# Forming each eight-block product of the late program in two halves, placed separately between the pairs of rows

## The chip, the cores and the metric

One core of one Trainium2 chip. The metric is the device time of one execution in microseconds (us). The engines are TensorE (PE for its matmuls, PEld for its weight loads), VectorE (DVE), ScalarE (ACT), GpSimd (POOL) and SyncE (SP), which issues most of the direct transfers.

## What is computed

One layer of an encoder over 1024 tokens of width 1024, all in fp32. What matters here is its last part, the "late" stage:

```
merged = sigmoid(gate_r) * (y_r @ w_proj_ret) + sigmoid(gate_s) * (y_s @ w_proj_sgu) + sigmoid(gate_a) * (y_a @ w_proj_att)
h = h + merged @ w_out
# PEER: 8 heads, 16 experts of 16384 for each head and token
act = gelu(einsum('thkd,td->thk', u_tab[eid], xt)); w = gate * act
h = h + einsum('thk,thkd->td', w, v_tab[eid])
h = h + sigmoid(rms_norm(h) @ ple_gate) * (p @ ple_proj)
```

The gates, `w_out`, the queries of PEER and `ple_gate` are products over a depth of 1024, which is eight blocks of 128.

## The kernel before

The 1024 tokens are eight tiles of 128, in three groups: tiles 0 and 1, tiles 2 to 4, tiles 5 to 7. Two earlier stages prepare keys and branches; then `late_stage` runs to the end and takes most of the time.

**Rows.** For each tile there are 128 selected experts for every token (8 heads times 16). One *row* r is one of these 1024 selections: GpSimd gathers 8 KB for each of the 128 tokens (`u` and `v` of the expert, 1 MB in all) into one of SLOTS = 11 buffers (L1218). VectorE forms the dot product with `u` (L1669), ScalarE the weight from it (L1493, L1497), and the weighted `v` is added either by VectorE (L1679) or by TensorE (L1344, four matmul records for a row, with a diagonal matrix made by ScalarE at L1501). TENSOR_ROWS says which: on TensorE 4 of 8 rows for tiles 0 and 1, 5 of 8 for tiles 2 to 4, 6 of 8 for tiles 5 to 7. GpSimd may gather row r only when row r - 11 has been added (`acc_done` or `acc2_done`), in the order of the rows.

**Slots.** `Plan` writes the order of every engine by hand. The late program is a list of slots; two rows, a *pair*, belong to each slot from `plan.first` = 35 on, so pair g is slot 35 + g, and there are 512 pairs. The dense products are *jobs*, each placed in a slot. In slot s each engine does, in this order:

- TensorE: the weighing (L1344) of pair s - 1, then the jobs of slot s.
- ScalarE: its part of the jobs of slot s - 1 (it reads their PSUM banks), its part of the search, then the weights of pair s.
- VectorE: its part of the jobs of slot s - 1 (`merge` L1585 and others), the dots of pair s, its weighing of pair s - 1, `finish` and `output` of a tile, then a part of the search (`search_keys` twice, `search_pairs`, `choose`, once in each eight slots).
- SP: the loads and stores whose conditions fall in slot s, in one queue.

A job of kind vs, us, gate, out, query or pgate has two chunks of weights of 1 MB each (`n_chunks` = 2) and takes eight blocks, all formed at one place by `matmuls` (L117, sixteen matmul records). A proj has one chunk and four blocks. The chunks stand in a ring of RING = 4 buffers; chunk n is loaded when the last job that uses chunk n - 4 has ended.

**Placement.** Up to the first rows, jobs are packed by PROLOGUE_US = 6.5 for each slot. Behind that `place` advances a position `at` by `job.us / rate[job.g]`, with `job.us` = 6.9 for an eight-block product and 3.5 for a proj; worked out, the rates are 6.5 for what is left of the first group, 3.99 for each slot in the second group and 2.45 in the third. `earliest` holds some kinds back by the slot of another job. The last products of a tile (hturn, pproj, pgate: `place_ple`, "the closing jobs of a tile" below) come after its last row, six slots for each tile.

Of the kernel before, what the change touches and what calls it, by code (L numbers as in the profile page):

```python
# [23 lines left out]
P = 128  # L24
S, D = 1024, 1024
T = S // P
DC = D // P
# [736 lines left out]
ACCS = 3  # L764
# [9 lines left out]
class Job:  # L774

    def __init__(self, kind, us, at, n_pa, n_pb, chunk, n_chunks, g=None, i=None, n=None, half=None, j=None, y=None, t=None):
        self.kind, self.us, self.at, self.slot = kind, us, at, None
        self.n_pa, self.n_pb, self.chunk, self.n_chunks = n_pa, n_pb, chunk, n_chunks
        self.pa, self.pb = (), ()
        self.g, self.i, self.n, self.half, self.j, self.y, self.t = g, i, n, half, j, y, t  # L780


class Plan:
# [22 lines left out]
    def count(self):  # L806

        self.jobs.sort(key=lambda job: job.slot)
        self.at = [[] for _ in range(self.n_slots)]
        n_pa = n_pb = 0  # L810
        for job in self.jobs:
            job.pa, n_pa = tuple(range(n_pa, n_pa + job.n_pa)), n_pa + job.n_pa
            job.pb, n_pb = tuple(range(n_pb, n_pb + job.n_pb)), n_pb + job.n_pb
            for k in range(job.n_chunks):
                self.last_job[job.chunk + k] = job
            self.at[job.slot].append(job)

    def take(self, source, *indices):
# [60 lines left out]
    def place(self):  # L879

        slot, used = 0, 0.0
        jobs = iter([job for job in self.jobs if job.t is None])
        start = self.of["score", 0, 1]
        for job in jobs:
            if used >= PROLOGUE_US or job.kind == "xt":
                slot, used = slot + 1, 0.0
            if self.earliest(job) > slot:
                slot, used = self.earliest(job), 0.0
            job.slot = slot
            used += job.us  # L890
# [12 lines left out]
        for job in rest:  # L903
            if job.g == 2:
                at = max(at, float(begin))
            at = max(at, float(self.earliest(job)))
            job.slot = int(at)
            at += job.us / rate[job.g]
        self.end = self.first + PAIRS
        self.n_slots = self.end + 10  # L910
        self.place_ple()
# [11 lines left out]
    def place_ple(self):  # L923

        free = 0
        for t in range(T):
# [3 lines left out]
            for half in range(2):  # L930
                self.of["pproj", t, half].slot = slot + 2
                self.of["pgate", t, half].slot = slot + 3 + half
            free = slot + 6

# [19 lines left out]
def late_stage(nc, A, R, X):  # L954


    plan = Plan()
    with ExitStack() as ctx:
# [66 lines left out]
        row_in = [sem(f"row{n}_in") for n in range(SLOTS)]  # L1025
        wp_in, pt_in, out_done = sem("wp_in"), [sem(f"pt{n}_in") for n in range(2)], sem("out_done")
        pa_done, pb_done = sem("pa_done"), sem("pb_done")
# [29 lines left out]
        def _(sp):  # L1057
# [72 lines left out]
            def load_h(t):  # L1130

                g = [n for n, group in enumerate(GROUPS) if t in group][0]
                i = GROUPS[g].index(t)
                sp.wait_ge(h_out[i], (nth(g, i) - (i < K0)) * 16)
                wait(sp, out_done, (t - ACCS + 1) * 32)
                sp.dma_start(acc[:, t % ACCS, :], X["h"][t]).then_inc(acc_in[t % ACCS], 16)
# [12 lines left out]
            def store_half(t, half):  # L1149
                hs = slice(half * HB, (half + 1) * HB)  # L1150
                sp.wait_ge(out_ready, 2 * t + half + 1)
                sp.dma_start(A["out"][t][:, hs], sum_of(t)[:, hs]).then_inc(out_done, 16)

# [14 lines left out]
            for s in range(plan.n_slots):  # L1168
# [30 lines left out]
                for n in range(len(PLE_TILES)):  # L1199
                    if s == plan.of["score", n + 1, 4 * len(GROUPS[n + 1]) - 1].slot + 1:  # L1200
                        load_wp(n)
            sp.wait_ge(out_done, T * 32)

# [23 lines left out]
        def _(pe):  # L1227
# [15 lines left out]

            def gate(job):
                if job.i == 0:
                    loaded(pe, job.chunk)
                    loaded(pe, job.chunk + 1)
                if job.kind == "vs":
                    wait(pe, xg_in[job.i], (nth(job.g, job.i) - (job.i < len(GROUPS[0]))) * 16)
                matmuls(pe, into_pa(job.pa[0])[:], [(xt[:, job.i, c * P:(c + 1) * P], wide_chunk(job.chunk, c)) for c in range(DC)]).then_inc(pa_done, 1)  # L1250

# [29 lines left out]

            def out(job):
                if job.i == 0:
                    loaded(pe, job.chunk)
                    loaded(pe, job.chunk + 1)
                for n in plan.of["turn", job.g, job.i].pb:
                    freed_pb(pe, n)
                matmuls(pe, into_pb(job.pb[0])[:], [(mt(job.i)[:, c * P:(c + 1) * P], wide_chunk(job.chunk, c)) for c in range(DC)]).then_inc(pb_done, 1)

# [3 lines left out]

            def query(job):
                if job.i == 0:
                    loaded(pe, job.chunk)
                    loaded(pe, job.chunk + 1)
                for n in plan.of["xt", job.g, job.i].pb:
                    freed_pb(pe, n)
                x = turned(job.g, job.i)  # L1300
                matmuls(pe, into_pa(job.pa[0])[:], [(x[:, c * P:(c + 1) * P], wide_chunk(job.chunk, c)) for c in range(DC)]).then_inc(pa_done, 1)

# [25 lines left out]

            def gate_product(job):
                loaded(pe, job.chunk)  # L1330
                loaded(pe, job.chunk + 1)
                for n in plan.of["hturn", job.t].pb:
                    freed_pb(pe, n)
                matmuls(pe, into_pa(job.pa[0])[:], [(ht[:, c * P:(c + 1) * P], wide_chunk(job.chunk, c)) for c in range(DC)]).then_inc(pa_done, 1)

            def weigh(r):
# [5 lines left out]
                for half in range(2):  # L1342
# [4 lines left out]
            query_of = {job.y: job for job in plan.jobs if job.kind == "query"}  # L1347
            qturn_of = {job.y: job for job in plan.jobs if job.kind == "qturn"}
            programs = {"vs": gate, "us": gate, "mix": mix, "yst": turn_gated, "gate": gate, "proj": proj, "turn": turn, "out": out, "xt": turn_normed, "query": query, "qturn": turn_query, "score": score,
                        "hturn": turn_sum, "pproj": project, "pgate": gate_product}  # L1350
# [481 lines left out]
```

## Time and profile before

| | |
|---|---|
| median of 3 runs | 3784.19 us (3777.92 to 3784.67) |
| the profiled execution's own time | 3773.32 us |
| its span | 3771.5 us |
| TensorE busy, share of the span | 82% |
| VectorE busy | 71% |
| bytes moved by DMA | 1281.06 MB, mean 340 GB/s |
| mean granted TensorE clock | 0.918 |

The span is that of the profiled execution, from the first to the last instruction. The dots (L1669) tell where a pair stands in time. Counted by them, these pairs begin at these times of the span:

| pair | 0 | 16 | 32 | 64 | 72 | 80 | 120 | 144 | 240 | 256 | 304 | 328 | 448 | 456 | 504 |
|---|---|---|---|---|---|---|---|---|---|---|---|---|---|---|---|
| us | 838.7 | 956.7 | 1052.3 | 1272.5 | 1326.0 | 1387.1 | 1621.8 | 1781.6 | 2322.5 | 2414.8 | 2677.9 | 2826.1 | 3423.0 | 3471.7 | 3703.7 |

The second group's gates and projections lie in pairs 20 to 68, its out products in 70 to 79; the closing jobs of tiles 0 and 1 in 120 to 132; the third group in 136 to 297, its out products in 234 to 250; the closing jobs of tiles 2, 3 and 4 in 305 to 324, those of tiles 5, 6 and 7 in 385 to 388, 449 to 452 and behind the last pair.

### The profile page before, as it was taken

To read this page: it belongs to the slowest core of one execution; us is meant where nothing else is said; L and a number is where in the kernel's file an instruction comes from. 1 tells how busy PE (TensorE), PEld (TensorE's weight loads), DVE (VectorE), ACT (ScalarE), POOL (GpSimd) and SP (SyncE) were. 2 spreads that over 40 slices of the span, in tenths; PEclk is the share of its full clock that TensorE was granted. 3 is DMA by queue.
4 is the path that set the end of the run, shared out by engine and by line. 5 is a ranking of instruction groups with operands and counts; after the bars stand their busy time and mean duration, and the time that the engine had idled before them with its cause. 6 is when DMAs were issued, how large, how long until landed. Compare 5 with 4: busy or idle time off the path is not lost. (4 is left out here: it accounts for less than half of the span.)

```text
span 3771.5 us, 31162 instructions
## 1 busy us (share of the span) xinstructions
PE 3078.5 (82%) x7880; PEld 1410.6 (37%) x7880; DVE 2671.1 (71%) x5254; ACT 1365.1 (36%) x3576; POOL 1198.4 (32%) x1092
## 2 busy tenths in 40 slices
PE   7889998988988989768988888798787677677676
PEld 4545554433433334323433333343332223223222
DVE  4356663136868778777888887877778878878884
ACT  3223332023443333344434433433453334334332
POOL 0000000013433334333544433443335444444442
PEclk9989998998999999888999999999898889889888
DMA  3321113459999999999999999999999999999996
GB/s 138 103 97 41 48 34 131 154 202 421 404 394 361 390 396 425 423 399 398 425 426 427 426 426 419 395 425 424 420 350 423 426 427 419 426 427 400 425 427 266
DMA packets 207881, 1281.06 MB, mean 340 GB/s; under 512 B 24048, under 2 KB 37616, under 8 KB 61936
## 3 DMA queue, kind: packets, MB, share of 16 engines
q0 software_dynamic: 147456, 1073.81, 68.7%
q1 hardware_dynamic: 55232, 195.61, 13.6%
q10 hardware_dynamic: 5040, 9.96, 0.7%
q8 instruction: 51, 0.84, 0.1%
q14 instruction: 102, 0.84, 0.1%
HBM read 1250.98 MB, written 28.31 MB: 339 GB/s over the span
## 5 line engine op out<-in xcount | busy, mean ns | idle before, releaser
L1344 PE MATMUL l_acc<-l_rows,l_diag 128*128 128x512 f32 x2624 | 1415.9, 684 | 600.3 <-ACT l_diag L1501 587.2
L1218 POOL DMA_INDIRECT l_rows<-in_peer_uv,l_at x1024 | 1177.7, 1150 | 1696.5 <-DVE l_acc L1679 846.0
L1344 PEld LDWEIGHTS l_acc<-l_rows,l_diag 128*128 128x128 f32 x2624 | 535.6, 214 | 1415.9 <-ACT l_diag L1501 857.1
L1669 DVE SCALAR_TENSOR_TENSOR l_rows<-l_rows,l_xn 128x1024 f32<-128x1024 f32 x640 | 762.9, 1223 | 142.3 <-DMA l_rows<-in_peer_uv,l_at 109.9
L1669 DVE SCALAR_TENSOR_TENSOR l_rows<-l_rows,all_xt 128x1024 f32<-128x1024 f32 x384 | 460.3, 1224 | 148.4 <-DMA l_rows<-in_peer_uv,l_at 125.0
L1493 ACT ACTIVATE l_dots<-l_dots 128x2 f32<-128x2 f32 x512 | 103.7, 203 | 1036.4 <-DVE l_rows L1669 1034.5
L1679 DVE SCALAR_TENSOR_TENSOR l_acc<-l_rows,l_wts,l_acc 128x1024 f32<-128x1024 f32 x272 | 349.5, 1285 | 98.2 <-ACT l_wts L1497 98.0
L117 PE MATMUL l_pa<-all_ring,all_xt 128*128 128x512 f32 x688 | 310.6, 603 | 4.5 <-PEq L71 4.5
L1497 ACT ACTIVATE l_wts<-l_dots,l_gates 128x1 f32<-128x1 f32 x1024 | 293.5, 287 | 16.8
L117 PE MATMUL l_pa<-l_ring,all_xt 128*128 128x512 f32 x656 | 293.8, 599 | 0.0
L1211 POOL CAST l_at<-l_expert 128x16 uint32<-128x16 f32 x64 | 20.5, 320 | 831.0 <-DVE l_expert L1655 830.8
L1501 ACT ACTIVATE l_diag<-all_ident,l_wts 128x128 f32<-128x128 f32 x656 | 263.5, 402 | 21.5
L117 PEld LDWEIGHTS l_pa<-all_ring,all_xt 128*128 128x128 f32 x688 | 133.8, 195 | 172.4 <-issue 172.4
L495 PE MATMUL b_p<-mix_w_branches,b_xnt 128*128 128x512 f32 x384 | 185.1, 636 | 10.5 <-DMA b_xnt<-kept_xnt 10.5
L117 PEld LDWEIGHTS l_pa<-l_ring,all_xt 128*128 128x128 f32 x656 | 126.5, 194 | 157.6 <-issue 157.6
L1493 ACT ACT_TABLE_LOAD x125 | 160.4, 1283 | 42.5 <-DVE l_rows L1669 41.3
L117 PE MATMUL l_pb<-l_ring,l_yt 128*128 128x512 f32 x320 | 144.6, 601 | 0.0
L117 PE MATMUL l_pb<-all_ring,l_yt 128*128 128x512 f32 x320 | 143.1, 597 | 0.0
L1679 DVE SCALAR_TENSOR_TENSOR l_merged<-l_rows,l_wts,l_merged 128x1024 f32<-128x1024 f32 x96 | 123.1, 1282 | 15.8 <-ACT l_wts L1497 15.8
L1390 ACT ACTIVATE l_sgk<-l_pa 128x512 f32<-128x512 f32 x48 | 28.7, 597 | 244.0 <-PE l_pa L117 243.9
L495 PEld LDWEIGHTS b_p<-mix_w_branches,b_xnt 128*128 128x128 f32 x384 | 76.5, 206 | 105.1 <-issue 86.8
L1629 DVE MAX8 l_top<-l_s_in 128x8 f32<-128x128 f32 x256 | 74.7, 292 | 41.0 <-DMA l_s_in<-kept_s 36.4
(262 smaller groups left out, 2893.1 us busy)
## 6 DMA issues: line engine op xcount, KB each, us to landing
l_ring<-in_w_late SPq DMA_DIRECT2D x54, 1024.0 KB, 9.0
all_ring<-in_w_late SPq DMA_DIRECT2D x54, 1024.0 KB, 8.8
l_rows<-in_peer_uv,l_at POOLq DMA_INDIRECT x1024, 17.3
kept_s<-l_yt ACTq DMA_DIRECT2D x32, 256.0 KB, 7.7
l_s_in<-kept_s SPq DMA_DIRECT2D x64, 128.0 KB, 7.0
mix_w_branches<-in_w_branches_kept SPq DMA_DIRECT2D x8, 768.0 KB, 4.8
k_x<-in_x SPq DMA_DIRECT2D x8, 512.0 KB, 6.0
k_w<-in_w_keys SPq DMA_DIRECT2D x2, 2048.0 KB, 10.7
```

Of the source, the lines that this page charges most:

```text
L117: last = pe.matmul(out, lhsT, rhs, start=(n == 0), stop=(n == len(pairs) - 1))
L495: last = pe.matmul(out[:], xnt[:, c, :], R["w_branches"][:, c, column:column + HB], start=(c == 0), stop=(c == DC - 1))
L1211: pool.tensor_copy(at[:, c % 2, :], expert[:, c % 3, :]).then_inc(at_ready, 1)
L1218: pool.indirect_dma_start(out=rows[:, r % SLOTS, :], out_offset=None, in_=A["peer_uv"], in_offset=bass.IndirectOffsetOnAxis(ap=at[:, c % 2 ...
L1344: ins = pe.matmul(acc2[:, hs], diag[n_pe(r) % DIAGS][:], rows[:, r % SLOTS, D + half * HB:D + (half + 1) * HB], start=first, stop=last)
L1390: act.activation(sg(job.i), pa[job.pa[0] % 2][:], ACT.Sigmoid).then_inc(pa_free[job.pa[0] % 2], 1)
L1493: act.activation(dots[:, n:n + 2], dots[:, n:n + 2], ACT.Gelu).then_inc(act_done, 1)
L1497: ins = act.mul(wts[:, m:m + 1], dots[:, m:m + 1], gates[:, c % 3, m:m + 1])
L1501: act.mul(diag[n_pe(r) % DIAGS][:], R["ident"][:], wts[:, m:m + 1]).then_inc(diag_ready, 1)
L1629: order(dve.max(values[:, eight], scores))
L1669: dve.scalar_tensor_tensor(out=u, in0=u, scalar=1.0, in1=xn_of(t), op0=ALU.mult, op1=ALU.mult, accum_out=dots[:, n:n + 1]).then_inc(dot_do ...
L1679: dve.scalar_tensor_tensor(out=sum_of(t), in0=rows[:, r % SLOTS, D:2 * D], scalar=wts[:, n:n + 1], in1=sum_of(t), op0=ALU.mult, op1=ALU.ad ...
```

## The change

Each eight-block job behind the first rows has a second place, `head`: its first four blocks, with the first chunk, are issued in slot `head`, its last four, with the second chunk, in `slot`. Where both fall in one slot the job is formed whole. `at` advances by half of the job's `us` for each half. In a slot the second halves are issued before the first ones. Whatever reads the product, releases its chunks or counts from its slot goes by `slot`, that of the second half. The closing jobs of a tile take eight slots in place of six. The count of finished output stores becomes one semaphore for each of the three `acc` buffers.

```diff
@@ Plan.count
+        for job in self.jobs:
+            if job.head is not None and job.head < job.slot:
+                self.tails[job.slot].append(job)
+                self.heads[job.head].append((job, True))
+            else:
+                self.heads[job.slot].append((job, False))
@@ Plan.place
-            job.slot = int(at)
-            at += job.us / rate[job.g]
+            if job.n_chunks == 2:
+                job.head = int(at)
+                at += job.us / 2 / rate[job.g]
+                job.slot = int(at)
+                at += job.us / 2 / rate[job.g]
+            else:
+                job.slot = int(at)
+                at += job.us / rate[job.g]
         self.end = self.first + PAIRS
-        self.n_slots = self.end + 10
+        self.n_slots = self.end + 12
@@ Plan.place_ple
-                self.of["pgate", t, half].slot = slot + 3 + half
-            free = slot + 6
+                self.of["pgate", t, half].head = slot + 3 + 2 * half
+                self.of["pgate", t, half].slot = slot + 4 + 2 * half
+            free = slot + 8
@@ SP
-                wait(sp, out_done, (t - ACCS + 1) * 32)
+                wait(sp, out_done[t % ACCS], t // ACCS * 32)
-                sp.dma_start(A["out"][t][:, hs], sum_of(t)[:, hs]).then_inc(out_done, 16)
+                sp.dma_start(A["out"][t][:, hs], sum_of(t)[:, hs]).then_inc(out_done[t % ACCS], 16)
-            sp.wait_ge(out_done, T * 32)
+            for n in range(ACCS):
+                sp.wait_ge(out_done[n], len(range(n, T, ACCS)) * 32)
@@ TensorE
+            def head(job, out, x, whole):
+                if job.i in (0, None):
                     loaded(pe, job.chunk)
+                for c in range(4):
+                    pe.matmul(out, x[:, c * P:(c + 1) * P], wide_chunk(job.chunk, c), start=(c == 0), stop=False)
+                if whole:
+                    return tail(job, out, x)
+
+            def tail(job, out, x):
+                if job.i in (0, None):
                     loaded(pe, job.chunk + 1)
+                for c in range(4, DC):
+                    last = pe.matmul(out, x[:, c * P:(c + 1) * P], wide_chunk(job.chunk, c), start=False, stop=(c == DC - 1))
+                return last
...
-                for job in plan.at[s]:
-                    programs[job.kind](job)
+                for job in plan.tails[s]:
+                    rests[job.kind](job)
+                for job, partly in plan.heads[s]:
+                    if job.n_chunks == 2:
+                        programs[job.kind](job, not partly)
+                    else:
+                        programs[job.kind](job)
```

`gate`, `out`, `query` and `gate_product` call `head` in place of `matmuls`, and each has a second function (`gate_rest` and so on) that calls `tail` and raises `pa_done` or `pb_done`.

## Rows read from the trace of the kernel before

**Rows 1.** The page: the span, and in 40 equal slices the DMA share and GB/s.

```profile
span 3771.5 us, 31162 instructions
...
DMA  3321113459999999999999999999999999999996
GB/s 138 103 97 41 48 34 131 154 202 421 404 394 361 390 396 425 423 399 398 425 426 427 426 426 419 395 425 424 420 350 423 426 427 419 426 427 400 425 427 266
```

**Rows 2.** Busy time in stretches; the last three columns are granted clock, DMA share, GB/s.

```profile
956.70:1052.30 95.60, 89.73 (x231) 40.83 (x230) 79.89 (x151) 39.87 (x100) 39.76 (x34) 0.98 0.98 403
1052.30:1272.50 220.20, 194.60 (x432) 82.91 (x430) 161.88 (x305) 83.45 (x197) 71.18 (x69) 0.97 0.96 371
1326.00:1387.10 61.10, 52.89 (x111) 21.97 (x109) 43.21 (x80) 21.16 (x53) 16.34 (x18) 0.92 0.97 381
1621.80:1781.60 159.80, 123.32 (x257) 52.23 (x256) 122.98 (x239) 74.05 (x178) 54.98 (x53) 0.88 0.98 394
1781.60:2322.50 540.90, 467.87 (x1066) 200.85 (x1065) 444.11 (x868) 217.92 (x580) 227.61 (x204) 0.96 1.01 426
2322.50:2414.80 92.30, 74.53 (x172) 31.48 (x171) 75.05 (x147) 41.45 (x108) 36.92 (x34) 0.91 0.96 388
2677.90:2826.10 148.20, 121.77 (x276) 52.75 (x275) 111.31 (x222) 77.53 (x189) 52.38 (x52) 0.94 0.95 374
2826.10:3423.00 596.90, 415.99 (x769) 161.90 (x768) 489.41 (x1012) 223.37 (x695) 282.02 (x256) 0.87 1.01 425
3423.00:3471.70 48.70, 41.44 (x97) 17.85 (x96) 36.32 (x74) 26.35 (x65) 17.02 (x18) 0.96 0.97 382
3703.70:3771.50 67.80, 48.79 (x104) 20.06 (x103) 28.63 (x42) 18.09 (x52) 11.89 (x9) 0.91 0.48 203
```

**Rows 3.** Waits in 1052.3 to 1272.5: engine line <- releaser: us, times, longest.

```profile
POOL l_rows L1218 <- DVE l_acc L1679: 107.5, 31, 7.6
...
ACT l_sgk L1390 <- PE l_pa L117: 53.8, 13, 8.1
...
POOL l_rows L1218 <- PE l_acc L1344: 29.8, 12, 4.7
```

**Rows 4.** Timeline of TensorE's matmuls from pair 49 to pair 53.

```profile
1169.81 3.60 PE L117 MATMUL l_pa<-l_ring,all_xt 128*128 128x512 f32 x8
1173.24 3.60 PE L117 MATMUL l_pa<-all_ring,all_xt 128*128 128x512 f32 x8
1176.67 1.88 PE L1344 MATMUL l_acc<-l_rows,l_diag 128*128 128x512 f32 x4
...
1192.03 3.60 PE L117 MATMUL l_pb<-all_ring,l_yt 128*128 128x512 f32 x8
1197.26 1.98 PE L1344 MATMUL l_acc<-l_rows,l_diag 128*128 128x512 f32 x4 [1.64 <-ACT l_diag L1501]
```

**Rows 5.** VectorE's first dots of pairs 51 and 52, in its timeline.

```profile
1186.78 1.23 DVE L1669 SCALAR_TENSOR_TENSOR l_rows<-l_rows,l_xn 128x1024 f32<-128x1024 f32 x1
...
1193.83 1.23 DVE L1669 SCALAR_TENSOR_TENSOR l_rows<-l_rows,l_xn 128x1024 f32<-128x1024 f32 x1
```

**Rows 6.** TensorE's matmuls of L117 in two stretches.

```profile
1052.30:1272.50 220.20, 135.63 (x304) 58.53 (x302) 0.97 0.96 371
1781.60:2322.50 540.90, 239.26 (x528) 103.39 (x528) 0.96 1.01 426
```

**Rows 7.** The same for L1344.

```profile
1052.30:1272.50 220.20, 66.42 (x128) 24.38 (x128) 0.97 0.96 371
1781.60:2322.50 540.90, 235.46 (x478) 90.35 (x477) 0.96 1.01 426
```

**Rows 8.** Chunk loads: the page's issue line, one pair's issue, the first product with it.

```profile
l_ring<-in_w_late SPq DMA_DIRECT2D x54, 1024.0 KB, 9.0
...
1700.38 0.81 SPq L1066 DMA_DIRECT2D all_ring<-in_w_late  x2
...
1725.01 6.17 PE L117 MATMUL l_pa<-all_ring,all_xt 128*128 128x512 f32 x14
```

More of the change, by code:

```diff
@@ L776, in __init__ @@
     def __init__(self, kind, us, at, n_pa, n_pb, chunk, n_chunks, g=None, i=None, n=None, half=None, j=None, y=None, t=None):
-        self.kind, self.us, self.at, self.slot = kind, us, at, None
+        self.kind, self.us, self.at, self.slot, self.head = kind, us, at, None, None
         self.n_pa, self.n_pb, self.chunk, self.n_chunks = n_pa, n_pb, chunk, n_chunks
@@ L816, in count @@
             self.at[job.slot].append(job)
+        self.tails, self.heads = ([[] for _ in range(self.n_slots)] for _ in range(2))
+        for job in self.jobs:
[4 more added lines that the diff above has]
+                self.heads[job.slot].append((job, False))
     def take(self, source, *indices):
@@ L1025, in late_stage @@
         row_in = [sem(f"row{n}_in") for n in range(SLOTS)]
-        wp_in, pt_in, out_done = sem("wp_in"), [sem(f"pt{n}_in") for n in range(2)], sem("out_done")
+        wp_in, pt_in, out_done = sem("wp_in"), [sem(f"pt{n}_in") for n in range(2)], [sem(f"out{n}_done") for n in range(ACCS)]
         pa_done, pb_done = sem("pa_done"), sem("pb_done")
@@ L1242, in turn8, with gate, gate_rest @@
                     last.then_inc(pb_done, 1)
-            def gate(job):
-                if job.i == 0:
+            def head(job, out, x, whole):
+                if job.i in (0, None):
                     loaded(pe, job.chunk)
+                for c in range(4):
[4 more added lines that the diff above has]
+                if job.i in (0, None):
                     loaded(pe, job.chunk + 1)
+                for c in range(4, DC):
+                    last = pe.matmul(out, x[:, c * P:(c + 1) * P], wide_chunk(job.chunk, c), start=False, stop=(c == DC - 1))
+                return last
+            def gate(job, whole):
                 if job.kind == "vs":
                     wait(pe, xg_in[job.i], (nth(job.g, job.i) - (job.i < len(GROUPS[0]))) * 16)
-                matmuls(pe, into_pa(job.pa[0])[:], [(xt[:, job.i, c * P:(c + 1) * P], wide_chunk(job.chunk, c)) for c in range(DC)]).then_inc(pa_done, 1)
+                last = head(job, into_pa(job.pa[0])[:], xt[:, job.i, :], whole)
+                if whole:
+                    last.then_inc(pa_done, 1)
+            def gate_rest(job):
+                tail(job, pa[job.pa[0] % 2][:], xt[:, job.i, :]).then_inc(pa_done, 1)
             def mix(job):
@@ L1280, in turn, with out, out_rest @@
                 turn8(job, lambda c: merged[:, job.i, c * P:(c + 1) * P])
[L1282 to L1285, printed above, removed]
+            def out(job, whole):
                 for n in plan.of["turn", job.g, job.i].pb:
                     freed_pb(pe, n)
-                matmuls(pe, into_pb(job.pb[0])[:], [(mt(job.i)[:, c * P:(c + 1) * P], wide_chunk(job.chunk, c)) for c in range(DC)]).then_inc(pb_done, 1)
+                last = head(job, into_pb(job.pb[0])[:], mt(job.i), whole)
+                if whole:
+                    last.then_inc(pb_done, 1)
+            def out_rest(job):
+                tail(job, pb[job.pb[0] % 4][:], mt(job.i)).then_inc(pb_done, 1)
             def turn_normed(job):
@@ L1292, in turn_normed, with query, query_rest @@
                 turn8(job, lambda c: scaled(job.g, job.i)[:, c * P:(c + 1) * P])
[L1294 to L1297, printed above, removed]
+            def query(job, whole):
                 for n in plan.of["xt", job.g, job.i].pb:
                     freed_pb(pe, n)
-                x = turned(job.g, job.i)
-                matmuls(pe, into_pa(job.pa[0])[:], [(x[:, c * P:(c + 1) * P], wide_chunk(job.chunk, c)) for c in range(DC)]).then_inc(pa_done, 1)
+                last = head(job, into_pa(job.pa[0])[:], turned(job.g, job.i), whole)
+                if whole:
+                    last.then_inc(pa_done, 1)
+            def query_rest(job):
+                tail(job, pa[job.pa[0] % 2][:], turned(job.g, job.i)).then_inc(pa_done, 1)
             def turn_query(job):
@@ L1327, in project, with gate_product, gate_product_rest @@
                 matmuls(pe, into_pb(job.pb[0])[:], [(p_t[:, job.t % 2, k, :], wp[:, k, hs]) for k in range(2)]).then_inc(pb_done, 1)
-            def gate_product(job):
-                loaded(pe, job.chunk)
-                loaded(pe, job.chunk + 1)
+            def gate_product(job, whole):
                 for n in plan.of["hturn", job.t].pb:
                     freed_pb(pe, n)
-                matmuls(pe, into_pa(job.pa[0])[:], [(ht[:, c * P:(c + 1) * P], wide_chunk(job.chunk, c)) for c in range(DC)]).then_inc(pa_done, 1)
+                head(job, into_pa(job.pa[0])[:], ht, whole)
+            def gate_product_rest(job):
+                tail(job, pa[job.pa[0] % 2][:], ht).then_inc(pa_done, 1)
             def weigh(r):
@@ L1348, in _ @@
             qturn_of = {job.y: job for job in plan.jobs if job.kind == "qturn"}
+            rests = {"vs": gate_rest, "us": gate_rest, "gate": gate_rest, "out": out_rest, "query": query_rest, "pgate": gate_product_rest}
             programs = {"vs": gate, "us": gate, "mix": mix, "yst": turn_gated, "gate": gate, "proj": proj, "turn": turn, "out": out, "xt": turn_normed, "query": query, "qturn": turn_query, "score": score,
```

## Prediction

> **What bounds the kernel now.** I read the page first: from the tenth slice on the DMA share is 9, and GB/s stands at 425 to 427 in most slices [rows 1]. 427 is the highest figure in any slice, and I take it as what the 16 DMA engines can do here. The bytes don't change with this edit, so in this part the kernel can get faster only where GB/s is under 427. The slices show where: 361 to 404 in slices 11 to 15, and single dips to 350, 395, 398 and 400 later [rows 1]. Then I cut the span at the dips. Time lost in a stretch is its length times (1 - GB/s / 427) [rows 2]:
>
> - A, pairs 16 to 79: 95.6 us at 403 lose 5.4; 220.2 at 371 lose 28.9; 61.1 at 381 lose 6.6. Sum 40.9.
> - B, pairs 120 to 143, closing jobs of tiles 0 and 1 and the third group's first products: 159.8 at 394 lose 12.4.
> - C, pairs 240 to 255, out products: 92.3 at 388 lose 8.4.
> - D, pairs 304 to 327, closing jobs of tiles 2 to 4: 148.2 at 374 lose 18.4.
> - E, pairs 448 to 455, closing jobs of tile 6: 48.7 at 382 lose 5.1.
>
> Sum 85.2 us. The third group's long stretch (540.9 us at 426) and the one mostly without products (596.9 at 425) lose about 4 together: there is nothing to win.
>
> Why do the DMA engines starve in these places? The waits say it: in 1052.3 to 1272.5 GpSimd, which issues the gathers, waits 107.5 us for VectorE's weighing and 29.8 us for TensorE's, so the 11 row buffers are full, not the queue [rows 3]. And what delays the weighing? A half of a product starts 3.43 us after the one before (1169.81 to 1173.24), so a whole product holds TensorE for 6.86 us between two pairs [rows 4]. ScalarE reads the product before it forms the next pair's weights, and waits 53.8 us for it [rows 3]; VectorE's weighing waits for those weights. Slots with a product take longer than the mean, slots without one shorter, and the ring cannot even them out fully.
>
> How far can stretch A's middle (32 pairs, 220.2 us, 6.88 for each pair) shrink? Two floors. DMA: 220.2 x 371 / 427 = 191.3 us. TensorE: 304 + 128 matmul records [rows 6, 7] of 3.43 / 8 = 0.429 us [rows 4] are 185.3 us at full clock, 191.0 at the granted 0.97 [rows 2]. Both are 5.98 us for each pair, against 6.88 now. So unevenness costs 29 us in this stretch, not work.
>
> **The change, part by part.**
>
> *Halves.* The placement can be followed from the rates. Of the 88 eight-block jobs behind the first rows (closing jobs apart), 78 fall in two slots and 10 stay whole, and the 16 of the closing jobs are all split. In the second group half a product advances the position by 3.45 / 3.99 = 0.87 of a slot, so nearly every slot gets one half or one projection: a weighing of four records, 4 x 0.429 = 1.72, and 3.43 make 5.15 us of TensorE, seldom 8.6; before, it was 8.6 with a whole product and 1.7 without one. In the third group halves are 1.41 slots apart.
>
> *Switching.* No work is added: the same matmuls, in groups of 8 records. The weighing starts 3.43 us after the half before it (1173.24 to 1176.67), just as a half does behind a half [rows 4], so a switch costs 0. Two ends: 0, and the 1.64 us that TensorE waits for a diagonal in such a place [rows 4] for each of 94 more switches, 154 us of TensorE. I take 0, because that wait exists only where TensorE has run ahead of the rows, which costs nothing while the DMA engines are busy.
>
> *What VectorE leaves.* Pairs 51 and 52 are 7.05 us apart (1186.78 to 1193.83) with TensorE waiting 1.64 us [rows 4, 5]: two dots, a weighing, a part of the search and a `merge` fill VectorE. Such pairs don't get shorter. Over 8 pairs VectorE is busy 161.88 / 4 = 40.5 us [rows 2] against 47.8 of the floors, so it is full in some pairs, not in the mean. I therefore stay above the floors: 6.25 us for each of the 32 pairs, 200 us, a saving of 20, or 0.7 of the loss. The same 0.7 for all of A gives 29 us. Bounds: 0.25 of it (only pairs with a product and no search) is 10; all of it is 41.
>
> *Closing jobs.* Before, two slots in succession held a whole product each; now four hold a half. TensorE's sum over them is the same, and more than the DMA engines need for so many pairs, so it still falls behind, but by less at a time. Other waits of these slots stay (the sum of the tile, its norm). I take 0.4 of D and E: 7.4 + 2.0. For B and C, where whole products at the third group's spacing are the cause beside that, 0.5: 6.2 + 4.2. Bounds for the four together: 0 and 44.
>
> *Chunks and stores.* A chunk's buffer is free only when the last tail is done, up to one slot later, for SP's load and all that is queued behind it (scores, later chunks, stores). In the second group the nearest reuse stays four slots off. The tightest is the third group's first chunks: released in slot 168 in place of 166, wanted in slot 171. Before, the load was issued at 1700.38 and used at 1725.01, 24.6 us later; a load lands in 9.0 us in the median [rows 8]. Three slots of 5.15 us or more still cover that, so 0; without cover TensorE would wait once for up to 9 us, and the 11 buffers take part of it. Output stores and loads of `h` move by one to three slots and nothing waits for them for tens of slots: 0. The three `out_done` semaphores add two waits at the very end, on transfers that are over: 0.
>
> *The end.* Behind the last pair nothing is left to alternate with; the same instructions run in the same order. The last 67.8 us (203 GB/s) [rows 2] stay.
>
> **Sum.** 29 + 6 + 4 + 7.4 + 2 = 48 us. The profiled execution's own time was 3773.3, so 3725. The median of the runs stands 10.9 us above that execution (3784.2), so I forecast 3736 us for the median, 1.3% faster. A difference of about 0.2% (7.6 us) is what a measurement of this kernel can tell from no change.
>
> **The rule that speaks against it.** In the stretch with few products the granted clock is 0.87, with products 0.96 or 0.97 [rows 2]; the two levels are 1.2 and 2.4 GHz, and the clock is low more of the time where TensorE idles between short pieces of work. The Trainium skill (TensorE: Matmul & The Clock Gate, "HAM oscillation — how this bites in real kernels") advises to keep all the blocks of a depth together before TensorE waits again, so that the clock stays up. Its rule would give the clock rival below. The trace agrees that idle stretches and a lower clock go together, but here the halves go into slots that had been idle.
>
> **Rivals.**
>
> *Everything is evened out.* All 85 us of the dips go: 3773.3 - 85 = 3688, 3699 as a median. For it: the floors of 5.98. Against it: pairs full on VectorE, and the waits around a tile's end.
>
> *VectorE is the bound in the dips.* Pairs like 51 (7.05 us) show it. Then A gains its lower bound, 10, and the rest a quarter of 44, 11: 21 us, 3763 as a median. Against it: VectorE's 40.5 us in 8 pairs that take 55.
>
> *Clock, the slower side.* If the products in short pieces bring the granted clock down, TensorE becomes the bound. The middle of A gets longer than now when 185.3 / clock is over 220.2, under a clock of 0.84; the third group's stretch, with 528 + 478 records [rows 6, 7] or 431.6 us at full clock, when it is under 431.6 / 540.9 = 0.80. At 0.78 the two cost 237.6 - 220.2 + 553.3 - 540.9 = 30 us: 3814 as a median. For it: 0.87 is seen where TensorE has little to do. Against it: idle stretches get shorter, not longer.
>
> *It only moves the loss.* Closing jobs of tiles 2 to 4 now take eight slots each in a row, and the halves meet search and `finish` in other slots; what A gains, B to E lose. No change: 3784.
>
> **How the numbers follow.** Forecast 0.50 (own range 3718 to 3755), all evened out 0.12, VectorE 0.18, loss moved 0.11, clock or another loss 0.09. The range goes from the first rival, 3700, to no change, 3784, and leaves about 0.15 outside. Faster by over 0.2%: 0.50 + 0.12 + 0.18 = 0.80; within it 0.11; slower 0.09.
>
> **What would show it.** GB/s over pairs 32 to 63 should rise from 371 to some 408 and the stretch should last about 200 us; GpSimd's 107.5 us of waits for VectorE's weighing should shrink, and ScalarE's 53.8 us for products by about half, with a granted clock of at least 0.96. D should last some 141 us. TensorE's L117 should show groups of 8 between groups of 4 of L1344. I am wrong if pairs without a search still take 7 us (another wait took over), if the clock in A is under 0.9, or if TensorE waits for a chunk around slot 171 or 56.

## The result, and the profile after

The changed kernel takes 3738.03 us in the median of 4 runs (3733.88 to 3739.56), the kernel before 3781.06 beside it (3776.82 to 3784.67). The ratio is 0.9891, 95% interval 0.9875 to 0.9906: 1.1% faster, 43 us. The profiled execution took 3739.03 us. The page of its profile, the span and the two rows that answer to [rows 1]:

```profile
span 3737.2 us, 31159 instructions
...
DMA  4321112449999999999999999999999999999995
GB/s 137 105 97 42 41 41 105 168 166 421 426 426 383 402 424 425 424 424 419 424 426 427 426 422 415 407 425 424 406 380 418 427 426 426 426 426 410 425 427 238
```

The plateau is the same 427. The dips at the eleventh to fifteenth slice have shrunk to two (383 and 402), the dip of 350 is one of 380. The same pairs as in [rows 2], by the dots of this kernel (busy time of PE, PEld, DVE, ACT, POOL, then granted clock, DMA share, GB/s):

```profile
957.80:1048.50 90.70, 87.61 (x230) 40.63 (x229) 81.78 (x156) 40.21 (x101) 36.16 (x35) 1.00 1.01 426
1048.50:1256.80 208.30, 188.54 (x425) 80.58 (x424) 161.51 (x305) 87.44 (x200) 71.78 (x69) 0.98 0.98 397
...
1306.60:1357.00 50.40, 49.26 (x115) 21.29 (x113) 41.70 (x79) 17.61 (x49) 17.91 (x17) 1.00 1.01 422
...
1599.10:1746.80 147.70, 121.50 (x256) 51.21 (x256) 121.09 (x236) 67.15 (x172) 54.00 (x52) 0.90 1.01 421
...
2287.00:2376.90 89.90, 70.45 (x161) 29.97 (x160) 76.08 (x149) 38.73 (x104) 38.39 (x35) 0.89 1.00 416
2376.90:2649.90 273.00, 224.06 (x579) 102.91 (x579) 210.01 (x416) 100.25 (x297) 112.53 (x103) 0.91 1.01 419
2649.90:2787.60 137.70, 111.06 (x252) 47.13 (x251) 108.53 (x218) 70.69 (x182) 54.25 (x52) 0.95 0.96 387
...
3386.90:3428.80 41.90, 38.50 (x92) 16.98 (x90) 34.68 (x71) 22.84 (x58) 16.80 (x17) 0.96 1.00 411
```

By the prediction's formula, length times (1 - GB/s / 427), the five dips lose now:

| dip | before [rows 2] | after | saved | forecast |
|---|---|---|---|---|
| A, pairs 16 to 79 | 40.9 | 15.4 | 25.5 | 29 |
| B, 120 to 143 | 12.4 | 2.1 | 10.3 | 6 |
| C, 240 to 255 | 8.4 | 2.3 | 6.1 | 4 |
| D, 304 to 327 | 18.4 | 12.9 | 5.5 | 7.4 |
| E, 448 to 455 | 5.1 | 1.6 | 3.5 | 2 |
| sum | 85.2 | 34.3 | 50.9 | 48 |

The two profiled spans differ by less, 34.3 us. By the same formula the stretches between the dips lose 17 us in place of 10 (the one between C and D, 273.0 us at 419 GB/s, loses 5.1 us where 263.1 at 425 lost 1.2). The first pair begins 4.2 us later (842.9 against 838.7); that is scatter, for three more profiles of kernels with the same plan up to there begin it at 836.3, 839.9 and 841.6. The end is 2.2 us longer (70.0 against 67.8). The profiled execution of before was 7.7 us under its median, the profiled one of after 1.0 over; so the medians differ by more than the profiles.

What ends the waits in pairs 32 to 63 of the changed kernel (the rows that answer to [rows 3]: engine, line, releaser: us, times, longest):

```profile
POOL l_rows L1233 <- DVE l_acc L1723: 106.1, 29, 10.3
...
ACT l_sgk L1434 <- PE l_pa L1273: 26.9, 9, 4.8
DVE l_sgk L1629 <- PE l_pb L117: 25.9, 3, 9.4
...
DVE l_merged L1627 <- PE l_pb L117: 9.0, 1, 9.0
DVE l_acc L1723 <- ACT l_wts L1541: 4.4, 2, 3.2
```

VectorE's waits in the same pairs of the kernel before:

```profile
DVE l_acc L1679 <- ACT l_wts L1497: 24.4, 6, 4.8
...
DVE l_sgk L1585 <- PE l_pb L117: 17.3, 3, 9.2
...
DVE l_merged L1583 <- PE l_pb L117: 9.1, 1, 9.1
```

ScalarE's wait for products has halved, 53.8 to 26.9 us, as forecast. What that wait does to the rows is seen in VectorE, whose weighing waits 4.4 us for ScalarE's weights in place of 24.4. GpSimd's wait for VectorE has not shrunk as the prediction said it should (107.5 to 106.1; its wait for TensorE's weighing went from 29.8 to 16.5), GB/s rose from 371 to 397 and not to 408, and the stretch lasts 208.3 us and not 200. And VectorE waits 34.9 us for projections, about 9 us each time, where it had been 26.4. The timeline shows where; first TensorE's matmuls, in the slots of pairs 48 to 50:

```profile
1157.18 3.60 PE L1264 MATMUL l_pa<-l_ring,all_xt 128*128 128x512 f32 x8
1160.62 1.88 PE L1382 MATMUL l_acc<-l_rows,l_diag 128*128 128x512 f32 x4
1162.33 3.60 PE L1273 MATMUL l_pa<-all_ring,all_xt 128*128 128x512 f32 x8
1165.77 1.88 PE L1382 MATMUL l_acc<-l_rows,l_diag 128*128 128x512 f32 x4
1167.48 3.60 PE L117 MATMUL l_pb<-all_ring,l_yt 128*128 128x512 f32 x8
```

And VectorE, which has nothing to do until the projection of 1167.48 is there:

```profile
1160.87 1.27 DVE L1723 SCALAR_TENSOR_TENSOR l_acc<-l_rows,l_wts,l_acc 128x1024 f32<-128x1024 f32 x1
1171.19 0.69 DVE L1629 TENSOR_TENSOR l_sgk<-l_pb,l_sgk 128x512 f32<-128x512 f32 x1 [9.04 <-PE l_pb L117]
```

A product's first half (L1264, at 1157.18) and its second (L1273, at 1162.33) stand apart with a weighing (L1382) between. The weighing starts 3.44 us behind the half, as a half behind a half did before (3.43), and the second half 1.71 us behind the weighing of four records (4 x 0.429 = 1.72): a switch costs nothing. But VectorE sits idle for 9.04 us. The dots and weighings of the next rows are queued behind its `merge`, though the rows have landed: the first of them, row 102, is in its buffer at 1155.6 us and its dot starts at 1172.64.

### The profile page after: what moved, and what is told of

Same layout as the page of the kernel before. It is cut to its first block and busy times, and to the rows that moved or that the text cites. A ratio compares the mean times of both kernels' runs of the same rounds, so it can differ in the third digit from the quotient of the medians.

```text
span 3737.2 us, 31159 instructions
## 1 busy us (share of the span) xinstructions
PE 3073.6 (82%) x7880; PEld 1411.8 (38%) x7880; DVE 2670.1 (71%) x5254; ACT 1365.2 (37%) x3573; POOL 1185.3 (32%) x1092
## 5 line engine op out<-in xcount | busy, mean ns | idle before, releaser
L1382 PE MATMUL l_acc<-l_rows,l_diag 128*128 128x512 f32 x2624 | 1418.5, 682 | 572.1 <-ACT l_diag L1545 564.2
L1382 PEld LDWEIGHTS l_acc<-l_rows,l_diag 128*128 128x128 f32 x2624 | 533.8, 213 | 1385.2 <-ACT l_diag L1545 821.6
L1537 ACT ACT_TABLE_LOAD x122 | 156.5, 1283 | 44.1 <-DVE l_rows L1713 43.1
L1273 PE MATMUL l_pa<-all_ring,all_xt 128*128 128x512 f32 x352 | 159.2, 595 | 0.0
L1264 PE MATMUL l_pa<-all_ring,all_xt 128*128 128x512 f32 x336 | 153.6, 600 | 4.5 <-PEq L71 4.5
L1264 PE MATMUL l_pa<-l_ring,all_xt 128*128 128x512 f32 x336 | 153.6, 600 | 0.0
L1273 PE MATMUL l_pa<-l_ring,all_xt 128*128 128x512 f32 x320 | 145.0, 596 | 0.0
L1629 DVE TENSOR_TENSOR l_sgk<-l_pb,l_sgk 128x512 f32<-128x512 f32 x32 | 22.1, 691 | 117.2 <-PE l_pb L117 113.5
L1673 DVE MAX8 l_top<-l_s_in 128x8 f32<-128x128 f32 x256 | 74.6, 291 | 39.5 <-DMA l_s_in<-kept_s 34.9
L1273 PEld LDWEIGHTS l_pa<-all_ring,all_xt 128*128 128x128 f32 x352 | 67.5, 192 | 85.3 <-issue 85.3
L1264 PEld LDWEIGHTS l_pa<-all_ring,all_xt 128*128 128x128 f32 x336 | 64.8, 195 | 84.1 <-issue 84.1
```

The source lines that it names most:

```text
L1264: pe.matmul(out, x[:, c * P:(c + 1) * P], wide_chunk(job.chunk, c), start=(c == 0), stop=False)
L1273: last = pe.matmul(out, x[:, c * P:(c + 1) * P], wide_chunk(job.chunk, c), start=False, stop=(c == DC - 1))
L1382: ins = pe.matmul(acc2[:, hs], diag[n_pe(r) % DIAGS][:], rows[:, r % SLOTS, D + half * HB:D + (half + 1) * HB], start=first, stop=last)
L1537: act.activation(dots[:, n:n + 2], dots[:, n:n + 2], ACT.Gelu).then_inc(act_done, 1)
L1629: evacuate(n, tt(part_sum, pb[n % 4][:], sg(job.i), ALU.mult))
L1673: order(dve.max(values[:, eight], scores))
```

## The experiments

The diffs show the deciding lines of each edit, against the changed kernel unless the text names another; lines that only follow from them are left out.

**Do the parts add up?** The changed kernel was run again beside three others.

> The changed kernel again, beside the next three, so that they can be compared with it on one chip. Both theories: 0.989 of the kernel before, within its interval of 0.9875 to 0.9906.

Measured: 3737.1 us, ratio 0.9894 (0.9879 to 0.9909).

Halves in the groups only:

```diff
-                self.of["pgate", t, half].head = slot + 3 + 2 * half
-                self.of["pgate", t, half].slot = slot + 4 + 2 * half
-            free = slot + 8
+                self.of["pgate", t, half].slot = slot + 3 + half
+            free = slot + 6
```

> Halves for the products of the groups; the closing jobs of a tile as before (whole, in two slots one behind the other, six slots for a tile). Mine, that each whole product of 6.9 us on TensorE between two pairs is what starves the gathers: A and C keep their gains of about 26 and 6 us, B, D and E lose part of their 20 us (B 10.6, D 5.4, E 3.6 measured), so some 3750 to 3757 us against 3781 before. Rival, that the gain in B, D and E comes from other things (a later start, chance): within 4 us of the changed kernel.

Measured: 3749.22 us, ratio 0.9922 (0.9909 to 0.9936), 29 us of the gain. Pairs 32 to 63 are exactly those of the changed kernel (208.3 us at 397 GB/s). D is worse than in the kernel before: 152.5 us at 352 GB/s, a loss of 26.8 in place of 18.4.

Halves and eight slots in the closing jobs only:

```diff
-            if job.n_chunks == 2:
-                job.head = int(at)
-                at += job.us / 2 / rate[job.g]
-                job.slot = int(at)
-                at += job.us / 2 / rate[job.g]
-            else:
-                job.slot = int(at)
-                at += job.us / rate[job.g]
+            job.slot = int(at)
+            at += job.us / rate[job.g]
```

> Halves and eight slots for the closing jobs of a tile only; the products of the groups whole and placed as before. Mine: A and C return to their losses of 41 and 8 us, E and D keep theirs, so 3762 to 3770 us. If the parts add up, the gains of this one and of the one with halves in the groups only sum to that of the change, 43 us.

Measured: 3762.36 us, ratio 0.9957 (0.9943 to 0.997), 16 us. Pairs 32 to 63 are those of before (220.4 us at 370). D loses only 6.3 us (135.1 us at 407), half of what it loses in the changed kernel. The two gains sum to 45 us against 41 for the changed kernel beside them: they add, within what the medians tell apart.

**Is it the division?** First, both halves at the place of the second:

```diff
-            if job.head is not None and job.head < job.slot:
-                self.tails[job.slot].append(job)
-                self.heads[job.head].append((job, True))
-            else:
-                self.heads[job.slot].append((job, False))
+            self.heads[job.slot].append((job, False))
```

> The placement of the changed kernel to the slot, readers, chunk loads and closing jobs included, but TensorE forms both halves together in the slot of the second. Mine: the halves themselves are the gain, so GB/s over pairs 32 to 63 falls back to 365 to 380 and the time to 3765 to 3790 us. Rival, that the places are the gain (readers one slot later, the closing jobs wider apart) and not the division: within 8 us of the changed kernel, 3732 to 3746 us.

Measured: 3826.18 us, ratio 1.012 (1.0105 to 1.0136), 48 us slower than before and slower than either theory said. Pairs 32 to 63 are much as in the kernel before (221.0 us at 367 GB/s); the rest of the loss is spread over the span, most plainly in pairs 72 to 79 (59.4 us at 327). Its waits for products in pairs 32 to 63:

```profile
ACT l_sgk L1432 <- PE l_pa L1269: 43.0, 12, 6.4
...
DVE l_sgk L1627 <- PE l_pb L117: 28.0, 3, 9.4
...
DVE l_merged L1625 <- PE l_pb L117: 10.9, 1, 10.9
```

The products stand whole and later, but their readers no later than in the changed kernel, so ScalarE and VectorE again read right behind them, as in the kernel before. (In one slot, that of pair 34, a product also shares the slot with a projection.) Which of this makes the kernel slower than the one before was not traced. At first the run seemed to speak for the division.

The other way round, both halves stand at the place of the first, while the readers stay where the change puts them. For 76 of the 88 products of the groups the first place is the old slot, for 12 it is one slot later. The closing jobs keep the places and the eight slots of the changed kernel:

```diff
+            first = job.slot if job.head is None else job.head
+            self.heads[first].append((job, False))
```

> The placement of the changed kernel, but TensorE forms both halves together in the slot of the first, which is where the whole product stood before; readers, chunk loads and the eight slots of the closing jobs stay as in the changed kernel. Mine, that the division is the gain: A keeps its loss of about 41 us (371 GB/s over pairs 32 to 63), only the wider closing jobs help, 3760 to 3785 us. Rival, that the gain is that readers and closing jobs stand later and wider: 3732 to 3746 us.

Measured: 3738.41 us, ratio 0.9893 (0.9876 to 0.9909), the changed kernel's time. My theory falls: with every product whole, and in pairs 32 to 63 each in its old slot, the gain is all there. It is not made up the same way. Pairs 32 to 63 take 212.0 us at 391 GB/s, 3.7 us more than with halves, while D takes 131.1 us at 413 and loses 4.3 us in place of 12.9, with the closing jobs whole in the very slots of the changed kernel. ScalarE's wait for products in pairs 32 to 63 is near that of the changed kernel:

```profile
DVE l_sgk L1628 <- PE l_pb L117: 29.4, 3, 11.1
...
ACT l_sgk L1433 <- PE l_pa L1270: 24.6, 8, 5.9
DVE l_merged L1626 <- PE l_pb L117: 9.1, 1, 9.1
```

Three kernels now stand side by side, the closing jobs apart. Products and readers in the old slots: 3781 us. Both later by the same slots: 3826. Products in the old slots (but for those 12) and readers later: 3738. The two kernels that read right behind a product are the slow ones, the one with more distance between them has the gain. So the new theory: what a product costs is not the 6.86 us for which TensorE is held, but the time for which an engine that handles rows waits for it in order. Halves shorten that wait (the reader stands behind 3.43 us instead of 6.86), and a later place of the reader does so as well.

**Reading later, with whole products.** The kernel before, with the products whole at their old place and the slot for readers, releases and dependents one later:

```diff
+            if job.n_chunks == 2:
+                job.head = int(at)
+                job.slot = int(at) + 1
+                at += job.us / rate[job.g]
```

> The kernel before with one thing changed: an eight-block product of the groups stays whole in its slot on TensorE, but its slot for all readers, releases and dependents is the next one. Closing jobs as before. Theory 'ScalarE's wait': what a whole product costs is that ScalarE waits for it ahead of the next pair's weights; to read it a slot later takes the wait away as well as two halves do. Then this is like the kernel with halves in the groups only, 3744 to 3754 us, with ScalarE's wait for products in pairs 32 to 63 at 30 us or less (53.8 before, 26.9 with the change). Rival 'evenness of TensorE': with whole products in the old places 3768 to 3782 us.

Measured: 3733.94 us, ratio 0.9881 (0.9859 to 0.9904); better than expected by the theory that was meant to win, without any halves and with the closing jobs whole and six slots apart as before (D still loses 18.5 us). The middle of A stands at the DMA plateau:

```profile
1044.10:1239.10 195.00, 184.92 (x423) 78.94 (x422) 162.55 (x305) 87.90 (x201) 76.78 (x69) 1.00 1.01 426
```

```profile
DVE l_sgk L1626 <- PE l_pb L117: 8.9, 3, 4.0
...
DVE l_merged L1624 <- PE l_pb L117: 4.2, 1, 4.2
...
ACT l_sgk L1431 <- PE l_pa L1268: 3.6, 2, 2.1
```

Whole products do not keep this stretch from its floor: TensorE is busy for 184.92 of 195.00 us, in lumps of 6.86, and the gathers stand at 426 GB/s. One reservation: since the second group starts six slots behind the last query's `slot`, everything in it also stands one slot later here, and so one place further in the search's cycle of eight pairs. The projections are read right behind their slot as before, so VectorE's wait for them (38.5 us in the kernel with whole products at the first place, 13.1 here) did not fall by reading them later relative to TensorE.

**Both together.** Halves, and readers one slot behind the second half (not for queries):

```diff
-                job.slot = int(at)
+                job.tail = int(at)
+                job.slot = job.tail + (job.kind != "query")
```

> The changed kernel, but for the products of the groups other than queries the slot for readers and releases is one behind the second half. Theory 'ScalarE's wait': its wait for products in pairs 32 to 63 falls from 26.9 to under 12 us, the stretch from 208.4 to some 203 us, the whole 2 to 8 us faster than the changed kernel. Rival, that TensorE's and the DMA engines' floors or VectorE hold that stretch by now: the wait falls, the time stays within 3 us.

Measured: 3729.69 us, ratio 0.9879 (0.9856 to 0.9902), the same as the one before within the intervals. ScalarE's wait fell to 9.3 us as expected, the stretch did not move, as the rival said:

```profile
1039.80:1248.20 208.40, 188.63 (x425) 80.59 (x424) 161.63 (x306) 89.17 (x202) 72.53 (x69) 0.98 0.99 403
```

```profile
DVE l_sgk L1630 <- PE l_pb L117: 30.0, 3, 10.7
ACT l_sgk L1435 <- PE l_pa L1274: 9.3, 3, 3.4
DVE l_merged L1628 <- PE l_pb L117: 7.7, 1, 7.7
```

VectorE shows why. Of its two waits, the one for ScalarE's weights was down to 4.4 us in the changed kernel, so ScalarE had little left to give; what is left is VectorE's wait for projections, 37.7 us. Is it the wait, or is VectorE full there? The changed kernel with the second add of each merge cut from 512 columns to 8 (that part of the branches' sum is left out):

```diff
-                    ins = tt(m, m, part_sum, ALU.add)
+                    ins = tt(m[:, 0:8], m[:, 0:8], part_sum[:, 0:8], ALU.add)
```

> The changed kernel with VectorE's second add of each merge cut from 512 columns to 8 (that part of the sum over branches is left out). If VectorE, full in the pairs with a merge and a search, is what still holds pairs 32 to 63 at 397 GB/s: that stretch goes from 208.4 us to under 204 and GB/s over 405, the whole 3 to 8 us faster. If TensorE with its clock, or the DMA engines, are the rest: 207 to 209 us as now.

Measured: 3736.4 us, ratio 0.9884 (0.9868 to 0.9901). The stretch takes 208.4 us against 208.3, with VectorE busy 157.05 us instead of 161.51: the nine adds take 166 ns each in place of 692. VectorE's waits for weights and projections grew by as much, from 39.3 to 43.9 us. These 4.5 us of its own work do not bound the stretch. Then the reading of projections was moved a slot later too, together with whole closing products that are read later and closing jobs sixteen slots apart, which lie outside this stretch:

```diff
+            elif job.kind == "proj":
+                job.head = job.tail = int(at)
+                job.slot = job.head + 1
+                at += job.us / rate[job.g]
```

> The one before, with the projections read a slot later too, the closing products whole and read a slot later, and the closing jobs of tiles 2 to 4 sixteen slots apart. If in-order waits for TensorE's products are what is left (ScalarE's, and VectorE's 25.9 us for projections in pairs 32 to 63), that stretch goes under 202 us and the whole to 3715 to 3728 us. If not, it is within 4 us of the kernel with the spread alone, 3735 us.

Measured: 3722.6 us, ratio 0.9854 (0.9833 to 0.9876), within the range expected. TensorE's places in pairs 32 to 63 are those of the halves that were read later; only VectorE's merges stand one slot later, and the stretch is at the plateau:

```profile
1041.50:1234.70 193.20, 184.82 (x422) 80.84 (x421) 163.03 (x305) 89.17 (x202) 74.17 (x69) 0.98 1.01 426
```

In-order waits in pairs 32 to 63, beside the time of the stretch, from the profile of each kernel. The second column is ScalarE's wait for products, the next two are VectorE's for ScalarE's weights and for projections, then the sum of these two (0 where the trace lists no such wait):

| kernel | ScalarE, products | VectorE, weights | VectorE, projections | VectorE, sum | stretch |
|---|---|---|---|---|---|
| before | 53.8 | 24.4 | 26.4 | 50.8 | 220.2 |
| whole at the second place | 43.0 | 13.0 | 38.9 | 51.9 | 221.0 |
| changed | 26.9 | 4.4 | 34.9 | 39.3 | 208.3 |
| changed, thin merge | 32.9 | 8.2 | 35.7 | 43.9 | 208.4 |
| whole at the first place | 24.6 | 4.6 | 38.5 | 43.1 | 212.0 |
| halves, read later | 9.3 | 0 | 37.7 | 37.7 | 208.4 |
| whole, read later | 3.6 | 0 | 13.1 | 13.1 | 195.0 |
| whole, read later, closing jobs in halves (last experiment) | 4.2 | 0 | 16.4 | 16.4 | 197.4 |
| halves, projections read later too | 4.3 | 0 | 4.7 | 4.7 | 193.2 |

The stretch goes with VectorE's sum (the thin merge takes 4.5 us of VectorE's work out and gets 4.6 us of wait in its place). It does not go with ScalarE's own wait: from 26.9 to 9.3 us nothing is gained.

**The closing jobs of tiles 2 to 4.** Two kernels move them apart, or to another place in the search's cycle:

```diff
-            free = slot + 8
+            free = slot + (16 if t > 1 else 8)
```

> The changed kernel with the closing jobs of tiles 2, 3 and 4 sixteen slots apart in place of eight. Theory 'too dense': the 13 to 14 us that D still loses come from three closings in a row, each slot's TensorE work standing above what the DMA engines need; spread out, pairs 304 to 360 lose under 5 us, some 8 us faster than the changed kernel. Theory 'wrong phase' (the closing jobs meet the heavy parts of the search, every eighth pair): each closing loses its 4 us wherever it stands, no change within 3 us.

Measured: 3734.86 us, ratio 0.9883 (0.9866 to 0.9899). D is 126.7 us at 409 GB/s, a loss of 5.3 in place of 12.9; the next stretch (606.4 us at 423) loses 5.7 in place of 4.2, for the closing jobs that went there: only those of tile 2 lie wholly in D now.

```diff
             slot = max(self.first + (t + 1) * NSEL // 2, max(queries) + 12, free)
+            if t > 1:
+                slot += (self.first - slot) % 8
```

> The changed kernel with the closing jobs of tiles 2, 3 and 4 moved up to the next slot with the same place in the search's cycle of eight as in the kernel before (the first of them in pair 313, then 321 and 329, in place of 308, 316 and 324), still eight apart. Theory 'wrong phase': the loss falls from 13 or 14 us to the 6.4 that stand in the kernel with halves in the closing jobs only, some 7 us faster than the changed kernel. Theory 'too dense': no change within 3 us.

Measured: 3735.31 us, ratio 0.9884 (0.9868 to 0.9901). D is 129.5 us at 406, a loss of 6.4, and the next stretch (604.6 us at 423) loses 5.7; the products of tile 4's closing jobs, in pairs 331 to 334, have left D too. D and the stretch behind it together lose 11.0 and 12.1 us in place of 17.1, so neither "too dense" nor "wrong phase" is excluded. In the medians both are 2 us from the changed kernel, which the intervals don't resolve; the 7 to 8 us that each theory expected for the whole did not come.

**The best of both.** Whole products read one slot later in the groups (placed by the same lines as in "Reading later, with whole products"), halves in the closing jobs, and those of tiles 2 to 4 sixteen slots apart:

```diff
+            if job.kind == "pgate":
+                self.tails[job.slot].append(job)
+                self.heads[job.head].append((job, True))
+            else:
+                first = job.slot if job.head is None else job.head
+                self.heads[first].append((job, False))
```

> Products of the groups whole and read one slot later (the kernel where pairs 32 to 63 stood at 426 GB/s), the closing products in halves over eight slots, as in the changed kernel, and those of tiles 2 to 4 sixteen slots apart. If the waits in order are the cost in the groups, and the lump on TensorE is the cost only in the closing jobs, the gains add: dips A and C under 4 us, B under 3, D some 5, E 2, and 3712 to 3724 us, as fast as the fastest so far (3722.6) or faster. If the whole products' lump still costs something somewhere in the groups: 3726 to 3740 us.

Measured: 3721.36 us, ratio 0.9858 (0.9842 to 0.9875), as fast as the fastest so far, 1.4% faster than the kernel before. It was not run beside the changed kernel (0.9891, 0.9875 to 0.9906); the ratios say 0.3% faster, and their intervals touch. Pairs 32 to 63 take 197.4 us at 426 GB/s, D 125.5 at 418, a loss of 2.6, with the closing jobs of tile 4 in the next stretch (607.4 us at 422, a loss of 7.1 in place of 4.2). C lost 3.0 and E 2.0, as expected; B lost 3.8, a little more.

## Why the prediction was right, and where its reason was not

The number was right: 3736 us forecast, 3738.0 measured, a gain of 48 us forecast and 43 measured. That the two lie within 2 us is in part luck: the kernel before took 3781.1 beside the changed one, not the 3784.2 that the forecast starts from, and the profiled spans differ by 34.3 us only. The bound was right: no slice on the page of any profile here is above 427 GB/s. By the formula the dips give 51 us against 48 forecast, of which the stretches between them take 7 back.

*Switching costs nothing*: right, 3.44 us from half to weighing (1162.33 to 1165.77).

*A, 29 us*: 25.5. The floor of 5.98 us for each pair was right too (193.2 / 32 = 6.04 was reached), but the term of 6.25 was too low for this change: it stands at 6.51.

*Halves even TensorE out*: this is the step of the mechanism that failed. The prediction said "so unevenness costs 29 us in this stretch, not work". Two whole-product kernels show otherwise: in the old places but read where the change reads them, the time is the changed kernel's; read one slot later everywhere, the stretch reaches the plateau in lumps of 6.86 us. What costs is the wait in order of the engines that handle rows. The prediction had that wait in hand, 53.8 us in ScalarE [rows 3], and said that VectorE's weighing waits for its weights (24.4 us), but took both to follow from the lump on TensorE. What halves alone are worth, with the readers in their places, is 3.7 us of this stretch (208.3 against 212.0) and nothing in the median.

*What VectorE leaves*: I named pairs full on VectorE (two dots, a weighing, search and `merge`) as what keeps A from its floor. Such pairs do stay at 7.04 us (51 and 52 in the changed kernel), but with 0.53 us less in each of nine merges the stretch stayed 208.4 us; with the merges one slot later it fell to 193.2. What remained was a wait of about 9 us in VectorE for the first projection of three: pair 50, with the wait of 9.04, takes 14.1 us. The halves made that wait longer, not shorter (26.4 to 34.9 us).

*Closing jobs*: B, C and E gave more than forecast, D less. B and C together lost 4.4 us in place of 20.8. In the third group halves were not needed for C: it loses 2.1 to 3.0 us in the three kernels with whole products that are read later. D's loss depends on where its three closings stand: 26.8 us when whole, six slots apart and the first two three pairs later than before; 12.9 in the changed kernel (14.4 in its second profile); 6.3 where halves began in the old slots (but for tile 3, two pairs later). With the closings whole in the changed kernel's slots D loses 4.3, so dividing them did not help there; E loses 4.4 that way and 1.6 with halves.

*Chunks*: cover held; TensorE has no wait for a chunk of the late program in the trace.

*The clock rival* did not come: the middle of A was granted 0.98 with halves and 0.97 before. With whole products that were read later it was granted 1.00, the higher level (2.4 GHz) throughout (0.99 in the last experiment). The rule cited from the Trainium skill ("TensorE: Matmul & The Clock Gate", "HAM oscillation — how this bites in real kernels") advises to keep all the blocks of a depth together so that the clock stays up. In this stretch dividing them did not lower it, but TensorE was idle for little of the time either way (25.6 of 220.2 us before, 19.8 of 208.3 after). What sets the small differences is not shown: the halves with projections read later were granted 0.98 while TensorE was busy 184.82 of 193.2 us, more of the time than where it was granted 1.00.

*Open*: how much of the gain of "whole, read later" is the reading and how much the shift by one pair in the search's cycle. In all three kernels that reach the plateau in pairs 32 to 63, VectorE's merges stand one pair further in that cycle than in the others; in the one with halves TensorE's places did not move, in the two with whole products they did. A kernel that shifts the second group by one slot and reads as before was not run. For D the same question stands between density and phase; the whole closings that lost 4.3 us in the changed kernel's slots show that neither alone makes its loss.

## What to carry to other kernels

When one engine's long job sits in a hand-written order, look at who reads its result and what is queued behind that reader, before dividing the job. A reader that stands one step later holds its buffer for one step more and costs a line of the plan, and here it gave as much as dividing every product did; halves, later readers and later projections together, with the closing jobs spread, gave 1.5% in place of 1.1%. Sum the in-order waits of the engine that frees most of the buffers (VectorE here); the time of the stretch followed that sum, not the evenness of the producer and not the waits of an engine one step up.

## What the runs showed of the hardware that was not expected

TensorE was busy 184.92 of 195.0 us (95%) in fp32 products while the 16 DMA engines stood at 426 GB/s, no less than the 425 of a stretch where TensorE was busy 70% of the time (415.99 of 596.9 us, in the kernel before). A product of TensorE can be left open between its halves while another accumulates: weighing and halves follow each other at 3.44 and 1.71 us, which is 0.43 us for each record, as within a half.

Moving the whole products by one slot or two, with the same work and the same readers, changed the whole from 0.9893 to 1.012 of the kernel before (3738.4 against 3826.2 us): the order of a plan alone is worth 2.3% here.
